# VectorE in place of TensorE for the small state space matrices of layer one

## The chip, the cores and the metric

One core of a Trainium2 chip runs the whole block. The metric is the device time in microseconds (us), median of the runs. TensorE (PE), VectorE (DVE), ScalarE (ACT), GpSimd (POOL) and the DMA queue of SyncE (SP) are five instruction streams that meet only at semaphores.

## The reference

One layer on 1024 positions of width 1024, all in float32:

```
x = x + 0.5 * swiglu(rms_norm(x, ff1_norm), w_gate, w_up, w_down)      # "layer one": FFN 1
h = rms_norm(x, mix_norm);  q, k, v, u = split(h @ w_in)
attn = banded_sink_attention(q, k, v, sink)
ssm:  lam_bar = exp(lam*dt);  b_bar = ((lam_bar - 1)/lam) * b         # 32 groups, 64 states, 16 channels
      states = scan(lam_bar, u @ b_bar);  y = Re(states @ c) + d*u;  gelu, GLU
x = x + concat(rms_norm(attn), rms_norm(ssm)) @ w_out
x = x + 0.5 * swiglu(rms_norm(x, ff2_norm), ...);  return rms_norm(x, final_norm)
```

The state space part is computed in 128 chunks of 8 positions. For it the kernel needs, out of the small parameters: the injection matrices E (b_bar times powers of lam_bar, one 128x128 matrix for each of 16 pairs of groups, real and imaginary), the output matrices CL (c times powers of lam_bar), and the rotation factors of each chunk (cosine and sine, `cs`).

## The kernel before

Every instruction's order is written out by hand, one list for each engine, with semaphores between them. Both FFNs are Strassen products: per FFN 8 opening quarters, then instances n = 2 to 21 of 7 products of 12 matmuls (3 for each operand tile: low times high, high times low, high times high), then `down` with 77 steps (7 products of 11 steps, 12 matmuls a step). ACT and DVE split each weight tile into a high and a low part ahead of its use, DVE also makes the Strassen sums. In `down` a ring of six slots is filled: at its step q DVE splits the tiles of step q + 4.

GpSimd does the small work beside FFN 1, in program order: its small loads (each parameter load waits for a certain product of TensorE), a chain of 128x16 operations for lam, then it waits for `ct_taken` and makes CL in 16 pieces that go to DRAM, then a loop of four batches. Each batch copies its operands to `cur`, computes E for four pairs into `EBb` (L3352 to L3354), a small operation `passed` (L3340), stores EBb to DRAM (L3356), waits for the landing, computes the rotation factors by doubling into the same EBb (L3359 to L3376), and stores them too (L3379). After the loop GpSimd adds the squares for the norm of the mixer (L3071), which `norm_sum(N_MIX, 0)` on TensorE (L1211) waits for at step 70 of `down`. ACT computes these squares, and takes the next one only when the add before last is done.

Turned matrices: c is turned by 8 TensorE transposes (`c_tiles`, L1386) before instance 10 and copied by ACT (`c_out`). E comes back from DRAM to `ebs` after FFN 1 in one load of SP (L1106) and is turned by 32 TensorE transposes (`transposes_e`, L1492) before input projections 4 and 5 of the mixer, and copied to `Et` by ACT (`e_out`, L2088). Projections run in the order IN_ORDER; `WITH_PE` and `WITH_ACT` say which small steps stand in front of, or in the middle of, which projection: K makes the kernel blocks, I injects (L1505, needs Et and u8), Y outputs. SP stores each tile of u and loads it back as `u8` (L1046) for the injection; the rotation factors `csn` (L1052) are loaded between these, each after a number of transposes of E.

Of the kernel before, what the change touches and what calls it, by code (L numbers as in the profile page):

```python
# [122 lines left out]
def taken_in(o):  # L123
# [7 lines left out]
WITH_PE = {(1, 1): steps("m1"), (4, 0): steps("E0 E1 E2 E3"), (5, 0): steps("E4 E5 E6 E7"), (6, 0): steps("K0"), (6, 1): steps("I0"),  # L131
# [3 lines left out]
WITH_ACT = {3: steps("e0 e1 e2 e3 W3"), 4: steps("e4 e5 e6 e7 W4"), 5: steps("k0 k1 W5"), 6: steps("k2 k3"),  # L135
# [18 lines left out]

ROUND = [((kind, 2 * b + i) if kind == "K" else (kind, b), 0 if kind == "K" else i)
         for kind, b in sum((WITH_PE[o] for o in sorted(WITH_PE)), []) if kind in "KEIY"
         for i in range(1 if kind == "E" else 2)]
# [266 lines left out]
def block_kernel(nc, x, ff1_norm, ff1_w_gate, ff1_w_up, ff1_w_down, mix_norm, w_in, sink, a_re, a_im,  # L424
# [85 lines left out]
    ebs = at("ebs", 64 * KB, [P, 2, NJ, P])  # L510
    csn = [at(f"csn{b}", (64 + 4 * b) * KB, [P, 2, 4, NC]) for b in range(4)]
# [7 lines left out]
    Et = at("Et", 162 * KB, [P, NJ, 2, P])  # L519
    Mt = at("Mt", 162 * KB, [P, NG, P])  # L520
# [48 lines left out]
    c_in = at("c_in", a_v + 2 * KB, [P, 2, 4, 2, NS])  # L569
    cl_st = at("cl_st", a_v + 2 * KB, [P, 2, 2, (T + 1) * GH])  # L570
    EBb = at("EBb", a_v + 2 * KB, [P, 2, 4, P])
    CT = at("CT", a_v + 6 * KB, [P, 2, NJ, GH])
    ptmp = at("ptmp", a_v + 8 * KB, [P, 2, 256])
    bc_tmp = at("bc_tmp", a_v + 8 * KB, [P, 2, NJ, GH])
# [74 lines left out]
    eb_d = nc.dram_tensor("eb_scratch", (P, 2, NJ, P), F32, kind="Internal").ap()  # L649
# [72 lines left out]
    ct_ready = sem("ct_ready")  # L722
# [6 lines left out]
    pool_chain = sem("pool_chain")  # L729
    eb_stored = sem("eb_stored")  # L730
    cl_stored = [sem(f"cl_stored{i}") for i in range(2)]
# [8 lines left out]
    eb_loaded = sem("eb_loaded")  # L740
# [4 lines left out]
    e_ready = sem("e_ready")  # L745
    e_taken = sem("e_taken")
# [94 lines left out]
    def _(sp):  # L841
# [263 lines left out]
        sp.wait_ge(eb_stored, 4 * 32 + 16)  # L1105
        sp.dma_start(ebs[:, :, :, :], eb_d).then_inc(eb_loaded, 16)  # L1106
# [12 lines left out]
        load_csn(1)  # L1119
# [62 lines left out]
    def _(pe):  # L1182
# [198 lines left out]
        def c_tiles():  # L1381

            pe.wait_ge(c_loaded, 64)
            for ri in range(2):
                for i in range(4):
                    last = nc.tensor.transpose(bank[6 + ri][:, i * P:(i + 1) * P],  # L1386
                                               c_in[:, ri, i, :, :].rearrange("p a s -> p (a s)"), ident[:, :])
                last.then_inc(ct_ready, 1)

# [52 lines left out]
        for n in range(2, N_INST):  # L1442
            if n == 10:
                c_tiles()
            instance(n)
        down(0, first_half(N_MIX))

        def round_free(kind, b, i=0):
# [11 lines left out]
            if kind == "K":  # L1460
                pe.wait_ge(k_taken, b + 1)
            elif kind == "E":
                pe.wait_ge(e_taken, b + 1)
# [21 lines left out]
        def transposes_e(b):  # L1485

            pe.wait_ge(eb_loaded, 16)
            round_free("E", b)
            for jj in range(2):
                for ri in range(2):  # L1490
                    m = 2 * jj + ri
                    last = nc.tensor.transpose(bank[round_bank("E", b)][:, m * P:(m + 1) * P],  # L1492
                                               ebs[:, ri, 2 * b + jj, :], ident[:, :])
            last.then_inc(e_ready, 1)

        def inject(b):

            pe.wait_ge(e_taken, 2 * b + 2)
# [108 lines left out]
        step = {"K": blocks_k, "E": transposes_e, "I": inject, "Y": outputs_y,  # L1607
# [139 lines left out]
    def _(act):  # L1747
# [216 lines left out]
        def ffn(w):  # L1964

            for n in range(N_INST * w + 2, N_INST * (w + 1)):
                if n == 10:
                    c_out()
                instance(n)
# [26 lines left out]

        def c_out():

            for ri in range(2):
                act.wait_ge(ct_ready, ri + 1)  # L2000
                for g2 in range(2):
                    r = slice(g2 * NS, (g2 + 1) * NS)
                    src = bank[6 + ri][r, :].rearrange("p (j g h) -> p g j h", g=2, h=GH)[:, g2]
                    act.activation(CT[r, ri, :, :], src, ACT.Copy).then_inc(ct_taken, 1)

# [58 lines left out]
        act.wait_ge(eb_stored, 4 * 32 + 16)  # L2064
# [18 lines left out]

        def e_out(b):
            act.wait_ge(e_ready, b + 1)
            if b == 0:
                wait_lo(act, 2 * KD)
            act.activation(Et[:, 2 * b:2 * b + 2, :, :],  # L2088
                           bank[round_bank("E", b)][:, :].rearrange("p (j r m) -> p j r m", j=2, r=2), ACT.Copy
                           ).then_inc(e_taken, 1)  # L2090
# [66 lines left out]
        step = {"k": k_out, "e": e_out, "y": y_out, "X": exponentials, "C": p_out, "O": o_out, "g": gelu,  # L2157
# [148 lines left out]
    def _(dve):  # L2306
# [341 lines left out]
        def instance(n):  # L2648
# [16 lines left out]

            ahead_sum(0)
# [4 lines left out]
            ahead(2)  # L2671
            gate_c12(n)
# [20 lines left out]

        def ffn(w):

            for n in range(N_INST * w + 2, N_INST * (w + 1)):
                if n == 7:
                    prepare()
                instance(n)
            down(w)  # L2700

        def x_out(t, kh=1):
# [3 lines left out]
                            ).then_inc(xt_dve, 1)  # L2706

# [354 lines left out]
    def _(pool):  # L3062
# [21 lines left out]
        def small_loads():  # L3084
# [31 lines left out]
        def load_c(n, a):  # L3116

            pool.dma_start(c_in[:, n, :, a, :], (c_re, c_im)[n][0].rearrange("(i g) h p -> (g h) i p", g=8)
                           ).then_inc(c_loaded, 16)
# [86 lines left out]
        tt(th, aim, dt, ALU.mult)  # L3206
        exp_parts(xr)
        load_b(1, 0)
# [42 lines left out]
        for k in range(1, T):  # L3251
            if k % 2:
                load_c(k // 4, k // 2 % 2)
# [50 lines left out]
        pool.wait_ge(ct_taken, 4)  # L3304
# [25 lines left out]
        with pool.Fori(0, NJ // 4) as i:  # L3330
# [7 lines left out]
            def passed():  # L3338

                pool.tensor_tensor(mark[:, :], unit[:, 0, 0, :], unit[:, 0, 0, :], ALU.mult)  # L3340

            pool.wait_ge(eb_stored, i * 32 + 16)
# [5 lines left out]
            q = [ptmp[:, n, 0:4 * GH].rearrange("p (j h) -> p j h", h=GH) for n in range(2)]  # L3348
# [12 lines left out]
            while n < NC:  # L3361
                v = [ptmp[:, m, 0:4 * n].rearrange("p (j c) -> p j c", j=4) for m in range(2)]
# [6 lines left out]
                if 2 * n < NC:  # L3369
                    a, b_ = ptmp[:, 0, 0:4], ptmp[:, 1, 0:4]  # L3370
# [121 lines left out]
```

## Time and profile before

| | us |
|---|---|
| median of 3 runs | 1590.37 (1590.2 to 1590.79) |
| profiled execution | 1590.72 |
| its span | 1588.9 |
| PE busy in it | 1580.6 |
| DVE busy | 1096.8 |
| ACT busy | 714.3 |
| POOL busy | 512.5 |

The span is the time from the first to the last instruction of the profiled execution. The granted TensorE clock is 1.00 in each stage, which is the 2.4 GHz level. FFN 1 lasts to about 654, the mixer to about 922, FFN 2 to the end. Times in rows are microseconds from the start of the span.

### The profile page before, as it was taken

To read this page: it belongs to the slowest core of one execution; us is meant where nothing else is said; L and a number is where in the kernel's file an instruction comes from. 1 tells how busy PE (TensorE), PEld (TensorE's weight loads), DVE (VectorE), ACT (ScalarE), POOL (GpSimd) and SP (SyncE) were. 2 spreads that over 40 slices of the span, in tenths; PEclk is the share of its full clock that TensorE was granted. 3 is DMA by queue.
4 is the path that set the end of the run, shared out by engine and by line. 5 is a ranking of instruction groups with operands and counts; after the bars stand their busy time and mean duration, and the time that the engine had idled before them with its cause. 6 is when DMAs were issued, how large, how long until landed. Compare 5 with 4: busy or idle time off the path is not lost.

```text
span 1588.9 us, 22029 instructions
## 1 busy us (share of the span) xinstructions
PE 1580.6 (99%) x7537; PEld 1305.3 (82%) x7537; DVE 1096.8 (69%) x1731; ACT 714.3 (45%) x1323; POOL 512.5 (32%) x938
## 2 busy tenths in 40 slices
PE   9999999999999999999999999999999999999998
PEld 7888888888888888888887888888888888888887
DVE  7966667766569886854369768766566666578766
ACT  7544343433334444532567544434344343344444
POOL 3005788877768778323030250000000000000000
PEclk9999999999999999999999999999999999999999
DMA  8253334433488545766631131433333333885443
GB/s 287 92 80 111 119 119 148 146 138 124 166 318 265 139 137 135 271 182 151 133 133 41 54 134 53 131 106 106 106 107 106 106 106 129 309 279 152 123 110 139
DMA packets 158455, 230.06 MB, mean 145 GB/s; under 512 B 25864, under 2 KB 95120, under 8 KB 154768
## 3 DMA queue, kind: packets, MB, share of 16 engines
q1 hardware_dynamic: 155120, 221.02, 43.6%
q0 software_dynamic: 3072, 7.62, 2.6%
q8 instruction: 61, 1.00, 0.3%
q14 instruction: 42, 0.34, 0.1%
q10 hardware_dynamic: 160, 0.07, 0.0%
HBM read 153.47 MB, written 74.15 MB: 143 GB/s over the span
## 4 chain that ended last, share of the span: by engine, by line
PE 98%; POOL 1%; ACT 0%; DMA 0%; DVE 0%; issue 0%; SPq 0%; DVEq 0%; POOLq 0%; ACTq 0%
PE bank L1185 31%; PE bank L1186 31%; PE bank L1187 31%; POOL ssq L3071 1%; PE bank L1552 1%; PE bank L1579 1%; PE bank L1534 0%; PE bank L1505 0%; PE bank L1479 0%; PE bank L1565 0%; PE bank L1527 0%; DMA x_in<-in_x_dram 0%; PE bank L1714 0%; PE bank L1219 0%; PE bank L1412 0%
## 5 line engine op out<-in xcount | busy, mean ns | idle before, releaser
L1185 PE MATMUL bank<-hbhi,ws_lo 128*128 128x512 f32 x1040 | 405.2, 390 | 0.0
L1187 PE MATMUL bank<-hbhi,ws_hi 128*128 128x512 f32 x1040 | 404.7, 389 | 0.0
L1186 PE MATMUL bank<-hblo,ws_hi 128*128 128x512 f32 x1040 | 404.6, 389 | 0.0
L1187 PEld LDWEIGHTS bank<-hbhi,ws_hi 128*128 128x128 f32 x1040 | 195.2, 188 | 40.7
L1185 PEld LDWEIGHTS bank<-hbhi,ws_lo 128*128 128x128 f32 x1040 | 195.2, 188 | 40.6 <-issue 0.4
L1186 PEld LDWEIGHTS bank<-hblo,ws_hi 128*128 128x128 f32 x1040 | 195.3, 188 | 40.3
L3071 POOL TENSOR_TENSOR ssq<-ssq,sqt 128x512 f32<-128x512 f32 x18 | 25.2, 1401 | 615.1 <-ACT sqt L1767 613.4
L1185 PE MATMUL bank<-d_hi,ws_lo 128*128 128x512 f32 x572 | 222.8, 389 | 0.0
L1187 PE MATMUL bank<-d_hi,ws_hi 128*128 128x512 f32 x572 | 222.5, 389 | 0.0
L1186 PE MATMUL bank<-d_lo,ws_hi 128*128 128x512 f32 x572 | 222.5, 389 | 0.0
L1837 ACT ACTIVATE loc<-bank 128x512 f32<-128x512 f32 x160 | 95.6, 597 | 251.6 <-PE bank L1187 251.6
L1884 ACT ACTIVATE d_hi<-d_in 128x512 fp32r<-128x512 f32 x154 | 96.0, 628 | 199.9 <-DMA d_in<-b_scratch 199.6
L2405 DVE TENSOR_TENSOR ws_lo<-w_sum,ws_hi 128x512 fp32r<-128x512 f32 x160 | 115.1, 719 | 97.3 <-ACT ws_hi L1800 97.3
L2575 DVE TENSOR_TENSOR d_lo<-d_in,d_hi 128x512 fp32r<-128x512 f32 x154 | 113.7, 740 | 82.9 <-ACT d_hi L1884 82.7
L1800 ACT ACTIVATE ws_hi<-w_sum 128x512 fp32r<-128x512 f32 x160 | 100.2, 626 | 76.2 <-PE bank L1187 60.1
L1185 PEld LDWEIGHTS bank<-d_hi,ws_lo 128*128 128x128 f32 x572 | 107.4, 188 | 22.7 <-issue 0.4
L1187 PEld LDWEIGHTS bank<-d_hi,ws_hi 128*128 128x128 f32 x572 | 107.4, 188 | 22.4
L1186 PEld LDWEIGHTS bank<-d_lo,ws_hi 128*128 128x128 f32 x572 | 107.4, 188 | 21.9
L1185 PE MATMUL bank<-hT_hi,w_lo 128*128 128x512 f32 x288 | 116.0, 403 | 0.0
L1186 PE MATMUL bank<-hT_lo,w_hi 128*128 128x512 f32 x288 | 112.4, 390 | 0.0
L1187 PE MATMUL bank<-hT_hi,w_hi 128*128 128x512 f32 x288 | 112.4, 390 | 0.0
L2405 DVE TENSOR_TENSOR ws_lo<-raw2a,ws_hi 128x512 fp32r<-128x512 f32 x78 | 55.0, 712 | 64.5 <-ACT ws_hi L1800 63.7
(319 smaller groups left out, 2696.6 us busy)
## 6 DMA issues: line engine op xcount, KB each, us to landing
b_scratch<-loc SPq DMA_DIRECT2D x42, 1024.0 KB, 7.3
d_in<-b_scratch SPq DMA_DIRECT2D x154, 256.0 KB, 3.1
raw2a<-in_ff_w_up_dram SPq DMA_DIRECT2D x42, 512.0 KB, 4.9
loc<-in_ff_w_gate_dram SPq DMA_DIRECT2D x36, 512.0 KB, 4.9
xT<-x_scratch SPq DMA_DIRECT2D x12, 1024.0 KB, 6.6
x_scratch<-xT SPq DMA_DIRECT2D x5, 2048.0 KB, 8.2
dw_lo_place<-in_ff_w_down_dram SPq DMA_DIRECT2D x8, 1024.0 KB, 7.9
x_in<-in_x_dram SPq DMA_DIRECT2D x8, 512.0 KB, 7.7
```

The lines of the kernel that those rows point to most:

```text
L1185: nc.tensor.matmul(o, wl, rh, start=first, stop=False, skip_group_check=chain)
L1186: nc.tensor.matmul(o, wh, rl, start=False, stop=False, skip_group_check=chain)
L1187: return nc.tensor.matmul(o, wh, rh, start=False, stop=last, skip_group_check=chain)
L1552: last = nc.tensor.matmul(o, qT[r, n, 2 * a:2 * a + 2, :].rearrange("p g q -> p (g q)"), kTp[r, n * CHUNK:n * CHUNK + P], start=True, stop ...
L1579: last = nc.tensor.matmul(bank[V_BANK[m]][kv * HD:(kv + 1) * HD, nn * 256:(nn + 1) * 256], vwin[:, 2 * m + nn, kv * HD:(kv + 1) * HD], pts ...
L1800: act.activation(as_block(ws_hi[b][:, :]), weights(n, s), ACT.Copy).then_inc(ws_hi_done, 1)
L1837: act.activation(snap[w][:, i, :], bank[inst_bank(n, role)][:, :], ACT.Copy).then_inc(snap_taken, 1)
L1884: act.activation(d_hi[q % N_SLOT][:, :], d_in[q % N_SLOT][:, :], ACT.Copy).then_inc(d_hi_done, 1)
L2405: dve.tensor_tensor(as_block(ws_lo[b][:, :]), weights(n, s), as_block(ws_hi[b][:, :].bitcast(F32)), ALU.subtract).then_inc(ws_lo_done, 1)
L2575: dve.tensor_tensor(d_lo[q % N_SLOT][:, :], d_in[q % N_SLOT][:, :], d_hi[q % N_SLOT][:, :].bitcast(F32), ALU.subtract).then_inc(d_lo_done, 1)
L3071: pool.tensor_tensor(ssq_of(norm, h), ssq_of(norm, h), sqt_of(norm, a), ALU.add).then_inc(ssq_done, 1)
```

## The change

VectorE turns c and E in blocks of 32x32, and what a full turn needs beyond that is done by the layout of the DMAs.

- c is loaded by 16 DMAs of 16 partitions and runs of 128 bytes in place of 4, and earlier in GpSimd's order (around `exp_parts(xr)` and no longer in the loop over k). DVE turns it in two instructions (`turn_c`) before its instance 8. TensorE's 8 transposes and ACT's copies are gone.
- In each of the four batches DVE turns EBb into a new tile EBt, two instructions of 128x512 (`turn_e`). GpSimd waits for them (`eb_turned`) and stores EBt by 4 DMAs of 32 partitions and runs of 128 bytes. It no longer waits for a store to land before the rotation factors. DVE does its turns at fixed places: before everything of instance 16; in instance 20 ahead of `gate_c12`; at step 21 and at step 52 of `down`. There it waits for `eb_made`.
- SP loads Et in 4 DMAs of 512-byte runs straight into its place; `ebs`, TensorE's 32 transposes and ACT's 8 copies are gone. The first two loads of rotation factors move ahead of `load_in(4)`.
- Et and Mt move to 64 KB, csn to 162 KB (they swap places); `csn` 2 waits for the norm's low parts. bc_tmp moves, ptmp has a second place in the loop.
- The parameter loads a_re, a_im and log_dt wait for earlier products: the last one for product 3 of instance 3 in place of product 3 of instance 4.

```diff
-WITH_PE = {(1, 1): steps("m1"), (4, 0): steps("E0 E1 E2 E3"), (5, 0): steps("E4 E5 E6 E7"), (6, 0): steps("K0"), ...
+WITH_PE = {(1, 1): steps("m1"), (6, 0): steps("K0"), ...
-WITH_ACT = {3: steps("e0 e1 e2 e3 W3"), 4: steps("e4 e5 e6 e7 W4"), ...
+WITH_ACT = {3: steps("W3"), 4: steps("W4"), ...
+E_TURN_INST = {16: (0, 0), 20: (1, 2)}
+E_TURN_STEP = {21: 2, 52: 3}
+E_STORES = 4 + 1
...
+    csn = [at(f"csn{b}", (162 + 4 * b) * KB, [P, 2, 4, NC]) for b in range(4)]
+    Et = at("Et", 64 * KB, [P, NJ, 2, P])
+    Mt = at("Mt", 64 * KB, [P, NG, P])
+    et_d = nc.dram_tensor("et_scratch", (32, NJ, 2, 4, P), F32, kind="Internal").ap()
...                                                            # SP
         def load_csn(b):
-            sp.wait_ge(e_ready, 4 if b == 0 else 8)
             if b:
                 sp.wait_ge(cs_loaded, 16 * b)
+            if b == 2:
+                wait_lo(sp, 2 * KD)
...
-        sp.dma_start(ebs[:, :, :, :], eb_d).then_inc(eb_loaded, 16)
+        for b in range(P // 32):
+            sp.dma_start(Et[32 * b:32 * b + 32, :, :, :], et_d[:, :, :, b, :]).then_inc(et_loaded, 16)
...
+        load_csn(0)
+        load_csn(1)
         load_in(4)
         store_u(0)
-        load_csn(0)
         load_u8(0)
         load_in(5)
         store_u(1)
-        load_csn(1)
         load_u8(1)
...                                                            # PE
-            if n == 10:
-                c_tiles()
...
         def inject(b):
-            pe.wait_ge(e_taken, 2 * b + 2)
+            pe.wait_ge(et_loaded, 64)
...                                                            # DVE
             for q in range(6 * N_PAIR):
+                if q in E_TURN_STEP and w == 0:
+                    turn_e(E_TURN_STEP[q])
...
+        def turn_e(b):
+            dve.wait_ge(eb_made, b + 1)
+            for ri in range(2):
+                dve.transpose(EBt[:, :, ri, :], EBb[:, ri, :, :]).then_inc(eb_turned, 1)
+        def turn_c():
+            dve.wait_ge(c_loaded, 16 * 16)
+            for ri in range(2):
+                dve.transpose(CT[:, ri, :, :]..., c_in[:, ri, :, :]...).then_inc(ct_taken, 1)
...                                                            # POOL
-                    pool.wait_ge(product_done, products(2 + n, 3 * g2))
+                    pool.wait_ge(product_done, products(2, 4 * n + 2 * g2))
-                pool.wait_ge(product_done, products(4, 3 * g2))
+                pool.wait_ge(product_done, products(3, 1 + 2 * g2))
...
+        load_c(0, 0)
+        load_c(0, 1)
         exp_parts(xr)
+        load_c(1, 0)
+        load_c(1, 1)
...
-            passed()
-            pool.dma_start(eb_d[:, :, bass.ds(i * 4, 4), :], EBb[:, :, :, :]).then_inc(eb_stored, 16)
-            pool.wait_ge(eb_stored, i * 32 + 32)
+            passed().then_inc(eb_made, 1)
+            pool.wait_ge(eb_turned, i * 2 + 2)
+            for a in range(P // 32):
+                pool.dma_start(et_d[:, bass.ds(i * 4, 4), :, :, 32 * a:32 * a + 32]..., EBt[32 * a:32 * a + 32]...
+                               ).then_inc(eb_stored, 16)
```

## Rows read from the trace of the kernel before

**Rows 1.** The page's busy times, and the waits of PE (in total, times, longest).

```profile
PE 1580.6 (99%) x7537; PEld 1305.3 (82%) x7537; DVE 1096.8 (69%) x1731; ACT 714.3 (45%) x1323; POOL 512.5 (32%) x938
...
PE bank L1211 <- POOL ssq L3071: 0.2, 1, 0.2
```

**Rows 2.** Timeline of PE where c is turned: start, duration, line, operands, count.

```profile
214.37 1.03 PE L1386 MATMUL bank<-ident,c_in 128*128 128x128 f32 x8
...
215.47 0.39 PE L1186 MATMUL bank<-hblo,ws_hi 128*128 128x512 f32 x1
```

**Rows 3.** Timeline of PE where E is turned, then the group by line.

```profile
676.97 0.39 PE L1187 MATMUL bank<-hT_hi,w_hi 128*128 128x512 f32 x1
677.20 1.91 PE L1492 MATMUL bank<-ident,ebs 128*128 128x128 f32 x16
...
679.18 0.39 PE L1186 MATMUL bank<-hT_lo,w_hi 128*128 128x512 f32 x1
...
L1492 PE MATMUL bank<-ident,ebs x32: 270/272/273, 677.2 to 686.1; 128*128 128x128 f32 x32
```

**Rows 4.** Timeline of POOL at the ends of batches, and its adds for the norm.

```profile
499.23 0.68 POOL L3356 DMA_DIRECT2D eb_scratch<-EBb  x1
503.16 0.84 POOL L3359 TENSOR_TENSOR EBb<-unit 128x8 f32<-128x8 f32 x1 [3.25 <-DMA eb_scratch<-EBb]
...
585.49 0.53 POOL L3340 TENSOR_TENSOR mark<-unit 128x1 f32<-128x1 f32 x1
...
590.32 0.69 POOL L3359 TENSOR_TENSOR EBb<-unit 128x8 f32<-128x8 f32 x1 [3.54 <-DMA eb_scratch<-EBb]
...
626.76 1.36 POOL L3071 TENSOR_TENSOR dw_hi_place<-dw_hi_place 128x512 f32<-128x512 f32 x1
...
631.68 1.57 POOL L3071 TENSOR_TENSOR dw_hi_place<-dw_hi_place 128x512 f32<-128x512 f32 x1
```

**Rows 5.** Timeline of PE at `norm_sum(N_MIX, 0)`.

```profile
634.46 0.60 PE L1211 MATMUL bank<-ident,dw_hi_place 128*128 128x128 f32 x4
```

**Rows 6.** Timeline of DVE around the four places where turns of E are put.

```profile
331.06 0.81 DVE L2387 TENSOR_TENSOR w_sum<-raw2a 128x512 f32<-128x512 f32 x1
...
415.20 0.69 DVE L2405 TENSOR_TENSOR ws_lo<-w_sum,ws_hi 128x512 fp32r<-128x512 f32 x1 [1.32 <-ACT ws_hi L1800]
...
502.05 0.68 DVE L2570 TENSOR_TENSOR ws_lo<-dw_lo_place,ws_hi 128x512 fp32r<-128x512 f32 x1
...
585.15 0.81 DVE L2570 TENSOR_TENSOR ws_lo<-dw_a,ws_hi 128x512 fp32r<-128x512 f32 x1
```

**Rows 7.** Groups by line: POOL's DMA issues (ns), and DVE's transpose of v.

```profile
L3356 POOL DMA_DIRECT2D eb_scratch<-EBb x4: 679/679/682, 341.4 to 586.1; - x4
...
L3113 POOL DMA_DIRECT2D b_raw<-in_b_im_dram x2 | 1.8, 894 | 1.2 <-POOL pw L3170 0.9 <-POOL pw L3166 0.3
...
L2799 DVE STREAM_TRANSPOSE vTp<-bank x2: 717/718/718, 743.8 to 753.2; 128x512 f32<-128x512 f32 x2
```

**Rows 8.** POOL's timeline after the parameter loads, and the page's DMAs (median us to landing).

```profile
130.81 0.82 POOL L3113 DMA_DIRECT2D b_raw<-in_b_re_dram  x1 [18.52 <-DMA par<-in_log_dt_dram]
...
b_raw<-in_b_re_dram POOLq DMA_DIRECT2D x2, 64.0 KB, 6.0
...
par<-in_log_dt_dram POOLq DMA_DIRECT2D x2, 4.0 KB, 17.6
```

**Rows 9.** The load of the second tile of u8, its injection on PE, and u8's landings.

```profile
691.29 4.50 SPq L1046 DMA_DIRECT2D u<-u_scratch  x8
...
701.41 1.97 PE L1505 MATMUL bank<-u,Et 128*64 128x128 f32 x32
...
DMA to landing us min/median/max: 2.0/2.6/4.3
```

**Rows 10.** Timeline of POOL: one operation of the loop beside an idle and a full DVE.

```profile
333.27 0.30 POOL L3353 TENSOR_TENSOR ptmp<-cur 128x64 f32<-128x64 f32 x1
...
579.75 0.63 POOL L3353 TENSOR_TENSOR ptmp<-cur 128x64 f32<-128x64 f32 x1
```

More of the change, by code:

```diff
@@ L152 @@
 STATE_STEPS = 4 * 5 + 8
+E_TURN_INST = {16: (0, 0), 20: (1, 2)}
+E_TURN_STEP = {21: 2, 52: 3}
+E_STORES = 4 + 1
 ROUND = [((kind, 2 * b + i) if kind == "K" else (kind, b), 0 if kind == "K" else i)
-         for kind, b in sum((WITH_PE[o] for o in sorted(WITH_PE)), []) if kind in "KEIY"
-         for i in range(1 if kind == "E" else 2)]
+         for kind, b in sum((WITH_PE[o] for o in sorted(WITH_PE)), []) if kind in "KIY"
+         for i in range(2)]
 def round_number(kind, b, i=0):
@@ L509, in block_kernel @@
     zT_lo = at("zT_lo", 48 * KB, [P, 4, L], F32R)
-    ebs = at("ebs", 64 * KB, [P, 2, NJ, P])
-    csn = [at(f"csn{b}", (64 + 4 * b) * KB, [P, 2, 4, NC]) for b in range(4)]
+    csn = [at(f"csn{b}", (162 + 4 * b) * KB, [P, 2, 4, NC]) for b in range(4)]
     yT = at("yT", 64 * KB, [P, 4, L])
@@ L729, in block_kernel @@
     pool_chain = sem("pool_chain")
+    eb_made = sem("eb_made")
+    eb_turned = sem("eb_turned")
     eb_stored = sem("eb_stored")
+    et_loaded = sem("et_loaded")
     cl_stored = [sem(f"cl_stored{i}") for i in range(2)]
@@ L1379, in x_tiles @@
                     last.then_inc(xt_done, 1)
[L1381 to L1388, printed above, removed]
         def first_half(norm):
@@ L1483, in blocks_k @@
                             last.then_inc(k_ready, 1)
[L1485 to L1494, printed above, removed]
         def inject(b):
-            pe.wait_ge(e_taken, 2 * b + 2)
+            pe.wait_ge(et_loaded, 64)
             pe.wait_ge(u8_loaded, 16 * T * (b + 1))
@@ L1605, in ssm_piece @@
             last.then_inc(mix_out, 1)
-        step = {"K": blocks_k, "E": transposes_e, "I": inject, "Y": outputs_y,
+        step = {"K": blocks_k, "I": inject, "Y": outputs_y,
                 "S": scores, "T": transposes_p, "V": weighted, "p": ssm_piece, "P": lambda i: ssm_piece(i, lambda: scores(i)), "m": lambda h: norm_sum(N_MIX, h), "n": lambda h: norm_sum(N_ATT, h),
@@ L1995, in x_out @@
                                ).then_inc(xt_act, 1)
[L1997 to L2004, printed above, removed]
         act.dma_start(ident[:, :], ident_c).then_inc(ident_loaded, 16)
@@ L2698, in ffn @@
                     prepare()
+                elif n == 8:
+                    turn_c()
                 instance(n)
@@ L2706, in x_out @@
                             ).then_inc(xt_dve, 1)
+        def turn_c():
+            dve.wait_ge(c_loaded, 16 * 16)
+            for ri in range(2):
+                dve.transpose(CT[:, ri, :, :].rearrange("p j h -> p (j h)"),
+                              c_in[:, ri, :, :].rearrange("p j s -> p (j s)")).then_inc(ct_taken, 1)
         def prepare():
@@ L3114, in load_b, with load_c @@
                            (b_re, b_im)[n][0].rearrange("(j g) p h -> g p j h", g=2)[g2]).then_inc(b_loaded, 16)
-        def load_c(n, a):
-            pool.dma_start(c_in[:, n, :, a, :], (c_re, c_im)[n][0].rearrange("(i g) h p -> (g h) i p", g=8)
-                           ).then_inc(c_loaded, 16)
+        def load_c(n, g2):
+            for sh in range(2):
+                for jj in range(2):
+                    q = 64 * g2 + 32 * sh + GH * jj
+                    pool.dma_start(c_in[q:q + GH, n, :, :],
+                                   (c_re, c_im)[n][0].rearrange("(j a g) h s -> a g h j s", a=2, g=2)[jj, g2][:, :, 32 * sh:32 * sh + 32]
+                                   ).then_inc(c_loaded, 16)
         def norm(which):
@@ L3347, in _ @@
                 ilink(pool.tensor_copy(cR[:, ri], rot8[:, ri, bass.ds(i * 4, 4)]))
-            q = [ptmp[:, n, 0:4 * GH].rearrange("p (j h) -> p j h", h=GH) for n in range(2)]
+            q = [ptmp_e[:, n, 0:4 * GH].rearrange("p (j h) -> p j h", h=GH) for n in range(2)]
             for t in range(T):
@@ L3361, in _ @@
             while n < NC:
-                v = [ptmp[:, m, 0:4 * n].rearrange("p (j c) -> p j c", j=4) for m in range(2)]
+                v = [ptmp_e[:, m, 0:4 * n].rearrange("p (j c) -> p j c", j=4) for m in range(2)]
                 w = [cR[:, m, :].unsqueeze(2).to_broadcast([P, 4, n]) for m in range(2)]
```

52 lines of the change are left out of this document (20 added, 32 removed).

## The prediction

> **What bounds the kernel now.** I read the page's busy times first. PE works 1580.6 us of a span of 1588.9 us, and the list of PE's waits has only one entry in the region of the change, 0.2 us for GpSimd's squares [rows 1]. So two questions decide: how much PE work goes, and whether anything that PE hardly waits for today becomes late. I then read PE's timeline at the removed transposes [rows 2, 3], and for each other engine the moment at which it hands over, against the moment at which PE asks [rows 4 to 6, 9].
>
> **What goes from PE.** The 8 transposes of c begin at 214.37, and the second matmul behind them at 215.47 [rows 2]. Without them it would begin one matmul spacing after 214.37. That spacing is 677.20 - 676.97 = 0.23 us [rows 3]. So they cost 1.10 - 0.23 = 0.87 us. For 16 transposes of E it is 679.18 - 677.20 - 0.23 = 1.75 us, and there are 32 [rows 3]: 3.50 us. Sum: 4.4 us. The mean duration of one (0.27 us) can't be used, as they overlap. ACT's 8 + 4 copies go too, worth nothing, since PE doesn't wait for ACT there.
>
> **What is added on DVE.** Eight transposes of 128x512 for E and two of 128x256 for c. The one of v took 0.72 us out of PSUM [rows 7]; back to back I take 0.65 each, so 1.3 us a batch. In the instances DVE has idle time (before the operation at 415.20 it sat 1.32 us waiting for ACT, [rows 6]), and in `down` the step it works on is used by PE four steps later. The work itself costs PE nothing. The waits of DVE for `eb_made` are the danger: behind the waiting turn stand all of DVE's splits, and behind these PE.
>
> **When GpSimd hands over.** The last parameter load moves by one instance (19 us by the spacing of instances, 7 x 12 x 0.23), and GpSimd stood 18.52 us for it before it went on at 130.81 [rows 8]. Sixteen loads of c in place of four cost it 7 to 10 us again (0.7 to 0.9 us an issue, [rows 7]). So it enters the loop some 10 us earlier, at least 7. The first batch was ready at 341.4 [rows 7] and would be at about 331; DVE arrives at 331.06 less the 0.9 us that PE has gained [rows 6]. From the first to the last batch GpSimd needs (586.1 - 341.4) / 3 = 81.6 us each [rows 7], and DVE's four places lie 84.8, 86.2 and 83.1 us apart [rows 6]. Thus DVE finds batches 1 and 2 ready, and GpSimd waits for DVE: it is from now on tied to DVE's places.
>
> **The last batch, step by step.** Turn 2 begins at 502.05 - 0.88 = 501.2, where GpSimd is ready at about 499.2 + 0.7, and ends at 502.5. Now come four store issues. The present one takes 0.68 us, one with 1024 short runs (b_raw) 0.89 [rows 7]: 2.7 to 3.8 us in all, and I take 3.0, nearer the store of the same loop. GpSimd begins the rotation factors at 505.6 where it did at 503.16 [rows 4]: 2.4 us later than before. Batch 3 would be made at 586.0 + 2.4 = 588.4 (585.49 and 0.53 for `passed`, [rows 4]). DVE is at its place at 585.15 - 0.88 = 584.3 [rows 6] and waits. While it waits, GpSimd's operations run at 0.30 in place of 0.63 us [rows 10]; with gaps and copies I take 1.6 times faster, so the last 4.1 us become 2.6 and the batch is made at 586.9. Turn 1.3, semaphore 0.1, stores 3.0: rotation factors from 591.3 where it was 590.32 [rows 4], 1.0 later. DVE then catches up and collides with GpSimd a little more, 0.3. So the adds for the norm begin 1.3 us later.
>
> **What that costs.** Four adds must be done before PE's `norm_sum`. They began at 626.76 and the fourth ended at 631.68 + 1.57 = 633.25 [rows 4]; PE came at 634.46 [rows 5]. The slack is 1.2 us, of which the earlier PE eats 0.9. So PE waits 1.3 - 0.3 = 1.0 us. Bounds: nothing, if the stores issue quickly and turns are short; and 4.1 us, with stores at 3.8 us and no gain in speed beside a waiting DVE (3.2 late after turn 2, 0.9 more at turn 3, 0.3 for collisions, less 0.3).
>
> GpSimd and VectorE slow each other here: the same operation of GpSimd took 0.30 us beside an idle DVE and 0.63 beside a full one [rows 10]. The Trainium skill (SBUF — State Buffer, Who interferes with whom) says that a VectorE instruction with two SBUF inputs contends with a reading GpSimd instruction, and one with a single SBUF input does not. By that rule the turns, with one input, take nothing from GpSimd, as in my sum; were it wrong, each batch would add at most the turns' 1.3 us to GpSimd, and only where GpSimd doesn't stand still for them anyway: the sum stays.
>
> **SP's queue.** Et comes in four loads where one stood, with CL and an input tile behind them. The projections asking for these lie 20 us off, so nothing. Rotation factors 0 and 1 leave the stretch between the u8 loads. The second tile of u8 was issued until 691.29 + 4.50 = 695.8 and lands 2.6 us after its issue, so at 698.4, and PE injected at 701.41 [rows 9]. PE now comes at 697.0. If the queue did not move, it would wait 1.4 us; but the two csn loads no longer stand in it and its own trigger, a projection of PE, moves as well, so I expect it 2 to 4 us earlier. Cost 0, bounds 0 and 1.4; the tiles behind it are alike, and a wait at one gives the others time.
>
> **Sum.** Profiled execution 1590.7 - 4.4 + 1.0 = 1587.3; it lay 0.35 above the median of the runs. Against that median: 1590.37 - 3.4 = **1587.0**. After the mixer nothing changes, and all of it is paced by PE.
>
> **Rivals.**
> - *Full gain.* GpSimd's adds are ready in time. For it: 1.2 us of slack today, and a DVE that waits speeds GpSimd up. Against: the four issues. 1586.0. Chance 0.30.
> - *The gain is given back.* Stores at 3.8 us, no speeding up, or waits for u8: 3 to 4.4 us of PE waits, 1589 to 1590.4. For it: in the last batches DVE is full beside GpSimd [rows 10]. Chance 0.17.
> - *Slower: the short stores hold the loop.* GpSimd enters the next batch only when all five stores of the last one have landed. The DMA of 1024 single values took 17.6 us to land, that of 1024 runs of 64 bytes 6.0 [rows 8]. If each of the four stores took 17.6 in turn, 70 us would pass where about 41 are there (36.4 us of rotation factors from 590.32 to 626.76, [rows 4], and some 5 for a landing), 29 us too much a batch; about 11 us are caught at the turns, and DVE, waiting at its places, would keep PE waiting: some 60 us, 1650. It decides from about 45 us for the four together; at 50 us it is 3 x 9 less what slack catches, some 16 us, and 1602. Against it: 4 x 6.0 = 24 us by the nearer row. A second way to this side is a first batch that comes 6 us late at instance 16, if the parameters land late. Chance 0.10.
> - *The change doesn't do what it says:* the transposes go in any case, and PE is nowhere idle beside them; I give it nothing.
>
> A rule that speaks for the slow side: the Trainium skill (DMA: Bandwidth & Descriptors, its table of figures at the head) wants at least 512 bytes a run and says that below it the DMA engine reads, modifies and writes. The new stores have 128. The trace has no such store; by the rule they'd be slower than today's store of 2 KB runs, which is the rival above.
>
> **Chances and range.** My own case (a wait of 0.4 to 3 us) has 0.43. Faster by over 0.2% means below 1587.2; 0.2% is about what a measurement of this kernel tells from no change. That holds for the full gain and for half of my case: 0.51. Slower (above 1593.5): 0.10. Within: 0.39. The range goes from 1585.6 (full gain, 0.4 for noise and easier queues) to 1591.2 (both bounds of the waits together, 4.1 and 1.4, would give 1591.5).
>
> **What would show it.** Right: no PE rows with `ident,ebs` or `ident,c_in`; two DVE STREAM_TRANSPOSE rows at each of four places near 330, 415, 501 and 587; GpSimd standing some 9 us before the second store, little before the others; DVE waiting 2 to 3 us for GpSimd at the last turn; the first add for the norm at about 628, and a wait of PE at its transposes for `norm_sum` of about 1 us. Wrong: a first add before 627 with no PE wait (full gain), or PE waits at an instance of FFN 1, at `inject`, or GpSimd's loop waiting over 8 us for stores to land.

## The result: slower, and by two waits of TensorE

| us | before | after |
|---|---|---|
| median of the runs | 1590.53 (1590.2 to 1590.79) | 1601.18 (1600.11 to 1603.34) |
| profiled execution | 1590.72 | 1600.11 |
| its span | 1588.9 | 1598.4 |

The ratio is 1.0069, with a 95% interval of 1.0056 to 1.0081. The prediction was 1587.0, in a range of 1585.6 to 1591.2. The profiled execution of the changed kernel is the fastest of its four runs; the account below is of that one, 9.4 us above before, where the medians lie 10.65 apart. The transposes are gone and PE's busy time is the same, which already says that some of the remaining work ran slower. PE's waits, the answer to [rows 1], name two places (in total, times, longest; "issue" means that the profile names nothing that PE waited for):

```profile
PE 1580.6 (99%) x7497; PEld 1304.6 (82%) x7497; DVE 1102.5 (69%) x1741; ACT 709.5 (44%) x1311; POOL 525.7 (33%) x962
...
PE bank L1218 <- POOL dw_hi_place L3056: 5.6, 1, 5.6
PE bank L1488 <- issue: 4.1, 1, 4.1
```

L1218 is `norm_sum` (L1211 before), L1488 is `inject` (L1505 before; `inject(b)` needs tile b of u8), L1473 makes the kernel blocks. PE's timeline around both, for [rows 5] and [rows 9]:

```profile
632.88 0.39 PE L1194 MATMUL bank<-d_hi,ws_hi 128*128 128x512 f32 x1
638.86 1.12 PE L1218 MATMUL bank<-ident,dw_hi_place 128*128 128x128 f32 x4 [5.59 <-POOL dw_hi_place L3056]
...
640.20 0.63 PE L1193 MATMUL bank<-d_lo,ws_hi 128*128 128x512 f32 x1
640.63 0.63 PE L1194 MATMUL bank<-d_hi,ws_hi 128*128 128x512 f32 x1
...
642.75 0.39 PE L1193 MATMUL bank<-d_lo,ws_hi 128*128 128x512 f32 x1
642.97 0.39 PE L1194 MATMUL bank<-d_hi,ws_hi 128*128 128x512 f32 x1
...
699.27 1.97 PE L1488 MATMUL bank<-u,Et 128*64 128x128 f32 x32
...
708.32 3.68 PE L1488 MATMUL bank<-u,Et 128*64 128x128 f32 x32 [4.13 <-issue]
711.93 3.10 PE L1473 MATMUL bank<-CL,Bb 64*16 64x128 f32 x32
```

Behind each wait the work runs at half speed for a while: matmuls 0.43 us apart until 642.3 and 0.23 from 642.75 on; an injection of 3.68 us where the one before it took 1.97. The stretches by time show it as the granted clock (the number behind the brackets; 0.5 is the 1.2 GHz level, 1.00 the 2.4 GHz level; the rows are the stretch behind each wait and the one after that):

```profile
638.80:643.00 4.20, 4.14 (x13) 3.45 (x14) 3.54 (x6) 3.01 (x7) 2.91 (x3) 0.53 0.01 2
643.00:647.00 4.00, 4.00 (x22) 3.30 (x20) 3.90 (x9) 3.67 (x7) 1.37 (x2) 1.00 0.48 124
...
708.30:715.00 6.70, 6.68 (x65) 5.46 (x65) 4.69 (x11) 0.00 (x0) 4.62 (x4) 0.55 0.64 176
715.00:719.00 4.00, 4.00 (x25) 3.11 (x25) 3.79 (x12) 0.96 (x2) 3.56 (x7) 1.00 0.89 222
```

With the start times of the same steps of PE in both timelines the whole difference comes apart (after less before, at each step):

| step on PE | before | after | difference | what happened since the step above |
|---|---|---|---|---|
| norm_sum(0) | 634.46 | 638.86 | +4.40 | c gone: -0.88 (measured in e14_sp_order below), wait: +5.28 |
| norm_spread(0) | 640.37 | 646.62 | +6.25 | lower clock: +1.85 |
| first kernel block | 691.73 | 694.43 | +2.70 | E gone: -3.55 |
| inject(1) | 701.41 | 708.32 | +6.91 | wait: +4.21 |
| inject(2) | 708.79 | 718.59 | +9.80 | lower clock: +2.89 |
| span | 1588.9 | 1598.4 | +9.5 | nothing of note |

So the gain of 4.4 us is there in full. Against it stand 9.5 us of waits, and 4.7 us of a halved clock behind them. (`norm_spread`, L1226, is the next step of the norm.)

**Why GpSimd was late.** Its timeline at the two last turns, for [rows 4], and the group of its store issues, for [rows 7]:

```profile
503.62 3.31 POOL L3349 DMA_DIRECT2D et_scratch<-EBt  x4 [3.67 <-DVE EBt L2668]
506.94 0.22 POOL L3353 TENSOR_TENSOR EBb<-unit 128x8 f32<-128x8 f32 x1
...
586.51 0.20 POOL L3331 TENSOR_TENSOR mark<-unit 128x1 f32<-128x1 f32 x1
588.75 1.62 POOL L3349 DMA_DIRECT2D et_scratch<-EBt  x2 [2.04 <-DVE EBt L2668]
594.31 1.56 POOL L3349 DMA_DIRECT2D et_scratch<-EBt  x2 [3.94 <-issue]
595.88 3.02 POOL L3353 TENSOR_TENSOR EBb<-unit 128x8 f32<-128x8 f32 x1
...
633.00 7.49 POOL L3056 TENSOR_TENSOR dw_hi_place<-dw_hi_place 128x512 f32<-128x512 f32 x5
...
L3349 POOL DMA_DIRECT2D et_scratch<-EBt x16 | 12.8, 804 | 18.4 <-DVE EBt L2668 14.0 <-issue 4.3
```

Up to 586.7 the timetable of the prediction holds. Then two things come that it has no term for: 3.94 us between the second and the third store, in which GpSimd waits for nothing that the profile names, and an operation of 128x8 that takes 3.02 us (0.69 before). The adds for the norm begin at 633.00.

**Why u8 was late.** SP's timeline, and the wait in it:

```profile
660.88 4.87 SPq L1113 DMA_DIRECT2D Et<-et_scratch  x4
...
671.26 14.30 SPq L1058 DMA_DIRECT2D csn<-cs_scratch  x2
685.61 0.60 SPq L851 DMA_DIRECT2D raw<-in_w_in_dram  x1
686.26 0.57 SPq L1041 DMA_DIRECT2D u_scratch<-ust  x1
693.37 3.64 SPq L1051 DMA_DIRECT2D u<-u_scratch  x8
...
702.73 3.63 SPq L1051 DMA_DIRECT2D u<-u_scratch  x8
...
SPq L1058 <- DMA csn<-cs_scratch: 12.4, 1, 12.4
```

`load_csn(b)` waits until csn b-1 has landed. Behind the four loads of Et (2 MB together), CL (2.3 MB), an input tile and 1 MB of parked x, csn 0 is waited for during 12.4 us, and the store of u, the input tile and both u8 loads stand behind that wait. The second u8 tile went out from 702.7 on (691.3 before, [rows 9]), though PE was to come earlier.

### The profile page after: what moved, and what is told of

The parts are those of the page before. It is cut to its first block, busy times and chain, and to the rows that moved or that the text cites. A ratio compares the mean times of both kernels' runs of the same rounds, so it can differ in the third digit from the quotient of the medians.

```text
span 1598.4 us, 21991 instructions
## 1 busy us (share of the span) xinstructions
PE 1580.6 (99%) x7497; PEld 1304.6 (82%) x7497; DVE 1102.5 (69%) x1741; ACT 709.5 (44%) x1311; POOL 525.7 (33%) x962
## 4 chain that ended last, share of the span: by engine, by line
PE 89%; POOL 6%; issue 2%; DMA 1%; POOLq 0%; DVE 0%; ACT 0%; SPq 0%; DVEq 0%; ACTq 0%
PE bank L1192 28%; PE bank L1194 28%; PE bank L1193 28%; POOL EBb L3362 1%; POOL ptmp_e L3361 1%; POOL ptmp_e L3360 1%; PE bank L1488 1%; PE bank L1535 1%; POOL ptmp_e L3343 1%; PE bank L1473 1%; POOL EBb L3345 1%; POOL ptmp_e L3344 1%; PE bank L1562 1%; PE bank L1517 0%; PE bank L1548 0%
```

## Experiments

Theory A: a VectorE that has waited at a turn catches up without a gap and starves GpSimd. Theory B: the wait of csn 1 for csn 0 in SP's queue makes u8 late. Their rivals: the four issues stall by themselves; the four loads of Et are what is late.

**Turn 3 a step later**

```diff
-E_TURN_STEP = {21: 2, 52: 3}
+E_TURN_STEP = {21: 2, 53: 3}
```

> The changed kernel with its last turn of E one step of `down` later (53 for 52). In the trace of the changed kernel DVE waited 2.8 us there, then worked 10.8 us without a gap, and in that stretch GpSimd stood 3.94 us between its second and third store and took 3.02 us for an operation of 128x8. Theory A: a VectorE that catches up without a gap starves GpSimd. At 53 DVE waits at most 1.3 us, catches up less, the two stalls shrink from 6.2 us together to under 3; the first add for the norm comes at 628 to 630 (633.0 in the changed kernel), PE waits 1 to 3 us at norm_sum (5.6): 1595.5 to 1598 us. Rival: four store issues in a row are what stalls (a queue that takes two). Then the 3.9 us gap stays, the first add comes at 631.5 or later and the time is at least 1599.5.

Measured: 1598.46 us (1596.81 to 1601.41), ratio to before 1.0056 [1.0039, 1.0073]. VectorE waited 1.2 us at its turns in all (4.1 in the changed kernel), the gap between store 2 and 3 stayed at 3.48 us, the first add came at 631.56. That is 1.4 us earlier than in the changed kernel, as the first operation behind the stores took 1.68 for 3.02 us. Theory A fails for the stall: the longer operation behind it may still be VectorE's doing. The time lies between the two ranges that were expected.

**csn 1 back**

```diff
         load_csn(0)
-        load_csn(1)
         load_in(4)
...
         store_u(1)
+        load_csn(1)
         load_u8(1)
```

> The changed kernel with the second load of rotation factors (csn 1) back behind store_u(1), as before the change. In the trace of the changed kernel SP stood 12.4 us for the landing of csn 0 before it could issue csn 1, and load_in(4), store_u(0), both u8 loads behind it. Theory B: this wait in the queue makes inject(1) wait 4.1 us, and the halved clock after it costs 2.9 more: without it u8 tile 1 is issued before 696, no PE wait at any inject, 7.0 us less: 1594 us (1593 to 1595). Rival: the four loads of Et (4.9 us of issue where one took 0.3) and their lateness are the cause: then inject(1) still waits 3 us or more and the time is 1598 or more.

Measured: 1594.50 us (1593.05 to 1598.64), ratio 1.0029 [1.0019, 1.0040], 6.7 us less than the changed kernel. inject(1) waits no more. New are 0.3 us at inject(2) and 1.4 us at inject(3). Theory B holds; the four loads of Et are still there, and inject(1) does not wait for them. Not all of the 6.7 us is this edit's. By the profiled runs, the changed kernel loses 6.8 us against before behind its first kernel block and this one 1.8, so 5.0 us are the edit's. The other 1.8 us lie ahead of that block, at norm_sum, which the edit doesn't touch: GpSimd's adds began at 631.33 here and at 633.00 there.

**Both**

> Both edits: turn 3 at step 53, csn 1 back. If both theories hold, and their effects add: 1588.5 to 1591 us, PE's only wait in the region that at norm_sum, 1 to 3 us. If either rival holds, 1592 or more.

Measured: 1594.46 us (1593.07 to 1596.15), ratio 1.0026 [1.0015, 1.0038], no better than csn 1 back alone, and above the 1588.5 to 1591 us that both theories together would give. GpSimd still stalled for 3.56 us; PE waited 3.1 us at norm_sum and 2.1 us at inject(3).

**VectorE only waits, in the kernel before**

```diff
+                if q == 51 and w == 0:
+                    dve.wait_ge(ct_taken, 4 + 4)
...
-            passed()
+            passed().then_inc(ct_taken, 1)
             pool.dma_start(eb_d ...
```

> The kernel before, in which DVE only waits, ahead of step 51 of `down`, until the last batch of E is made, some 3 to 4 us; no turn, one store as before. Theory A (a DVE that catches up starves GpSimd): DVE then works without a gap for over 8 us, GpSimd shows one or two idle stretches or operations of over 2 us in it, the first add for the norm comes at 628 or later (626.8 before) although the batch itself is made 1 to 1.5 us earlier, PE waits 1 us or more at norm_sum: 1591.5 to 1594. Rival (the four store issues stall by themselves): GpSimd has no such stretch, the first add comes at 625 to 626.5, time 1590.2 to 1590.8.

Measured: 1590.63 us (1590.30 to 1591.19), ratio 1.0001 [0.9991, 1.0010]. It tested nothing: in the profiled run GpSimd had made the last batch at 581.6, and VectorE shows no wait for it, though the same code made it at 586.0 in the kernel before. That is a finding of its own: GpSimd's loop is over 4 us earlier or later in one build than in another that gives it the same work, and the slack of 1.2 us that the prediction counted is one draw. A second pair shows it too: the changed kernel and e2_csn1_back differ only in SP's order from 671 us on, and the first batch was made at 331.3 and at 325.1. Some 4 us of this is one wait for a store of CL to land (6.81 us and 2.81) just ahead of the loop.

**One issue more, four issues less, 1024 runs more, code moved**

```diff
 e5: d_skip loaded in two halves in place of one
 e6: +pool.dma_start(par[:, n, :], a[0].rearrange("(j g) p -> (g p) j", g=2)), b likewise; turn 3 at 53, csn 1 back
 e10: +pool.dma_start(spare[:, :], a_re[0].rearrange("(j g) p -> g p j", g=2)[0])
 e11: +for _ in range(6): ilink(pool.tensor_tensor(ptmp_e[:, 0, 0:1], ...))      # ahead of the stores
```

> The changed kernel in which one small early load of GpSimd (d_skip, at 36 us) is split into two: one DMA issue of GpSimd more, everything else alike. In all traces with the turns GpSimd stands 3.5 to 3.9 us before the third store of the last batch, which is its 80th DMA issue (20 small loads and zero stores, 6 parameters, 4 of b, 16 of c, 16 of CL, 5 a batch, 2). Theory C: GpSimd's DMA issue number 80 has to wait until the ones just before it have landed. Then the stall moves to between the first and the second store of the last batch, and keeps its 3.5 to 4.5 us. Rivals (a VectorE without gaps; the place in the code; the bytes or runs issued so far, which don't change): the stall stays between the second and the third store.

> Turn 3 at step 53 and csn 1 back (as in e3_both), and GpSimd's two loads each of a_re, a_im, b_re and b_im made into one each: four issues of GpSimd fewer, the same bytes and runs. Theory C (by count): the last batch never reaches the 80th issue, no idle stretch over 1 us between its stores, the first add for the norm comes at 626.5 to 628.5 (631.0 in e3_both), PE waits under 1 us at norm_sum and its clock stays at the upper level; inject(3) still waits 1.5 to 2.5 us: 1587.5 to 1590 us. Rivals (by runs, by place, by VectorE): the 3.6 us stall stays, 1593 us or more.

> The changed kernel with one more early load of GpSimd of 1024 single values into an unused place, so that 1024 more runs have passed through its queue before the last batch. Splitting a load with no more runs did not move the stall, nor did four issues fewer with the same runs. Theory D' (a ring that holds so many runs, and waits at its end for those on the way): the stall moves one store (1024 runs) up, to between the first and the second store of the last batch, at 3.5 to 4.5 us. Rival (place in the code, or the state of the other engines at that moment): it stays between the second and the third.

> The changed kernel with six small operations of GpSimd more ahead of the first store of each batch (0.2 to 0.6 us each, 2 to 3.5 us a batch). Theory F (GpSimd waits for its own instructions: a boundary in the code lies between the second and the third store): the stall of 3.5 to 4 us moves to an earlier place in the order, before the second store or ahead of it. Theories of the queue (runs, landing): it stays between the second and the third store.

Measured (one run each; e6 ten): 1600.67; 1594.05 (1592.19 to 1595.89, ratio 1.0020 [1.0010, 1.0029]); 1598.12; 1602.18 us. In all four the stall lay between the second and the third store of the last batch, and nowhere else: 4.17, 3.27, 3.68 and 3.82 us. So theory C (the 80th issue), theory D' (a ring that fills up by runs, as far as single values count in it) and theory F (a boundary in GpSimd's code) fall for this stall. e11 also shows what a late GpSimd costs: add at 636.03, a wait of 8.1 us. The median of e6 is 0.4 us below that of e3_both, far less than either spreads (3.7 and 3.1 us); what GpSimd wins is lost again at its turns, where it now waits for VectorE for 23.7 us in all (14.0 in the changed kernel).

**Wide runs**

```diff
-                pool.dma_start(et_d[:, bass.ds(i * 4, 4), :, :, 32 * a:32 * a + 32].rearrange("c j r b s -> c (j r b) s"), ...
+                pool.dma_start(et_d[:, bass.ds(i * 4 + a, 1), :, :, :].rearrange("c j r b s -> c (j r b s)"),
+                               EBt[32 * a:32 * a + 32, :, :, :].rearrange("c j r m -> c (j r m)")
```

> The changed kernel with GpSimd's four stores a batch in runs of 4 KB in place of 128 bytes (same four issues, same bytes; the blocks land in the wrong order, so the output matrix E is not the reference's). Theory D (the number of short runs decides): no stall before the third store of the last batch (3.5 to 4.2 us in all traces so far), landing as quick or quicker, first add for the norm 3 to 4 us earlier than the 632.6 to 633.0 us of the changed kernel. Rival (place in the code, or a VectorE without gaps): the stall stays at 3.5 us or more.

Measured (one run): 1592.61 us. GpSimd's timeline in this run, and its group of issues:

```profile
588.09 2.27 POOL L3349 DMA_DIRECT2D et_scratch<-EBt  x4 [2.00 <-DVE EBt L2668]
...
626.80 8.17 POOL L3056 TENSOR_TENSOR dw_hi_place<-dw_hi_place 128x512 f32<-128x512 f32 x5
...
L3349 POOL DMA_DIRECT2D et_scratch<-EBt x16 | 8.2, 511 | 23.1 <-DVE EBt L2668 22.1
```

No gap between the stores, an issue of 0.51 in place of 0.80 us, the first add at 626.80, and no wait at norm_sum. (The 4.2 us at inject(1) remain, since csn 1 is where the change put it.) The short runs are a condition of the stall (with them the issues are longer too, so which of the two counts is not shown). They also take longer to land: 4.1 us in the middle against 3.2.

The Trainium skill (DMA: Bandwidth & Descriptors, the table of figures at its head) asks for runs of at least 512 bytes. Here 128-byte runs did cost, but at the engine that issues them, and only a little in the landing; the rival that took landings of 17.6 us, from the row of single values, was off by four times.

**As many short runs more as a batch has**

```diff
+        for a in range(P // 32):
+            for jh in range(2):
+                pool.dma_start(et_d[:, 2 * jh:2 * jh + 2, :, :, 32 * a:32 * a + 32] ..., Bb[32 * a:32 * a + 32, ...] ...
```

> The changed kernel with 4096 more short runs of 128 bytes (eight stores of 512 runs, to places that the first batch overwrites) issued by GpSimd just ahead of its loop: as many as a batch has. With wide runs the stall was gone; extra issues, extra single values and shifted code did not move it. Theory G (short-run stores fill something up, and the 14th thousand of their runs meets its end): the stall of 3.5 to 4 us now lies in batch 2 (near 505 us), between its second and third store, or thereabouts, and none is at 590 us. Rival H (what counts is the moment near 590 us: what else is in the queues and on VectorE, with short runs): it stays in the last batch. VectorE may wait for the first batch here, so the time is of no use (1600 to 1612 us).

Measured (one run): 1599.91 us. The stall stayed in the last batch (3.53 us, 591.0 to 594.55). Theory G falls. A much smaller gap does move. In the changed kernel GpSimd stands 0.32 us before the second store of the second batch; with a batch's worth of short runs more (this run), the same gap lies before the second store of the first batch:

```profile
417.93 2.34 POOL L3349 DMA_DIRECT2D et_scratch<-EBt  x3 [0.32 <-issue]
...
336.77 2.33 POOL L3356 DMA_DIRECT2D et_scratch<-EBt  x3 [0.31 <-issue]
```

One issue more or four less (e5, e6) leave it where it was. With 1024 single values more (e10) it is gone from there, and the first store of that batch begins 0.5 us later (417.29 for 416.76), one store earlier. So this gap, and not the stall, goes by the number of runs, single values included; it costs 0.3 to 0.5 us once.

What the changed kernel's trace does show is when the stall ends. The DMA rows of 592.5 to 593.5, then those of 593.5 to 595.0 (q0 is GpSimd's queue; packets, MB, share):

```profile
q0 software_dynamic: 27, 0.05, 15.6%
...
q1 hardware_dynamic: 137, 0.25, 61.7%
```

The last packets of the first two stores pass by 593.5, from then on q0 is empty, and the third store is issued at 594.31. It is the same in all ten traces with the stall: the last packet of GpSimd's queue passed 0.75 to 1.5 us before the third store was issued. In batch 2, in contrast, the third store was issued while nearly all packets of the first two were still to come. GpSimd thus goes on when its own queue has run dry. The stall also moves with the stores: they began between 586.8 and 595.0 in these kernels, and it came each time 1.6 us later.

**Turns placed by GpSimd's needs; then the stores on SP's queue**

```diff
 e7 (on e6): +turn 1 after ahead(1) in place of ahead(2);  E_TURN_STEP = {20: 2, 52: 3}
 e12 (on e7): -GpSimd's stores of EBt
+        def store_et(b):                                                       # SP
+            sp.wait_ge(eb_turned, 2 * b + 2)
+            for a in range(P // 32):
+                sp.dma_start(et_d[:, 4 * b:4 * b + 4, :, :, 32 * a:32 * a + 32]..., EBt[32 * a:32 * a + 32]...).then_inc(et_stored, 16)
+        # after pair 18, the first group for `down`, steps 26 and 58;  DVE waits for et_stored, 64 * b, before turn b
```

> As e6, with turn 1 two VectorE operations earlier in instance 20 (after its second weight), turn 2 at step 20, turn 3 at step 52. GpSimd stood 6.2 and 3.7 to 5.7 us for these turns. It should be some 2.7 us earlier from turn 1 on. Theory: no PE wait at norm_sum, first add at 624 to 626.5; the only PE wait left is at inject(3), 1.5 to 2.5 us, without a drop of the clock: 1587 to 1588.5 us. If VectorE has to wait at an earlier place instead, first add as in e6 and the same time as e6.

> As e7_turns_earlier, with the four stores of E a batch issued by SP's queue in place of GpSimd (after pair 18, after the first group for `down`, after steps 26 and 58). GpSimd loses 3.3 us of issue a batch and the stall of 3.5 us. Theory: first add for the norm at 623 (ACT's squares set it), no PE wait at norm_sum, clock never halved there; what is left is inject(3), 1 to 2.5 us: 1586.5 to 1588 us, a spread of the runs under 1.5 us (6.3 us in e7). Rival: 5 us of issue in SP's queue in `down` make d_in late, and PE waits there: 1589 or more.

Measured: e7 1590.63 us (1587.43 to 1593.71), ratio 1.0001 [0.9992, 1.0011]. GpSimd was 1.9 us earlier at its last stores than in the changed kernel (586.81), stalled for 3.45 us all the same, and PE waited 2.3 us, where no wait was expected: as fast as before the change, but with a spread of 6.3 us. VectorE sat idle for 0.54 us in the middle of this stall (590.29 to 590.83), and GpSimd did not go on: one more sign against theory A. e12: 1587.67 us (1586.48 to 1590.10), ratio 0.9981 [0.9972, 0.9991], first add at 623.96, no wait at norm_sum. The runs still spread by 3.6 us, where under 1.5 was expected. SP takes 2.7 to 3.3 us for the four stores of batches 1 to 3 (7.2 for batch 0), and no load for `down` came late. What was left is at inject(3), here in its profiled run (1590.10 us, the slowest of ten):

```profile
723.43 2.83 PE L1503 MATMUL bank<-u,Et 128*64 128x128 f32 x32 [2.12 <-issue]
```

**SP's order around the last tile of u**

```diff
-        load_csn(3)
         store_k(0)
         load_in(6)
+        load_csn(3)
+        store_u(3)
+        store_k(1)
         load_m(0)
-        store_k(1)
-        store_u(3)
-        load_in(7)
         load_u8(3)
+        load_in(7)
         load_m(1)
```

> As e12_sp_stores, with SP's queue reordered around the last tile of u: csn 3, store_u(3) and store_k(1) ahead of the first load of M, load_in(7) behind the last load of u8. In e12 SP issued the last u8 tile at 717.3 to 720.9, though u was ready at 709.6, and inject(3) waited 2.1 us and ran at a lower clock for 0.9. Theory: the tile is issued 1 to 1.5 us earlier, inject(3) waits under 1 us: 1586 to 1587.2 us, median of e12 less 0.5 to 1.5. Rival: the moved load_in(7) or load of M makes a later projection or output wait: 1587.7 or more.

Measured: **1586.43 us** (1585.53 to 1588.17), ratio to before 0.9974 [0.9964, 0.9984]: 4.3 us less than 1590.75, the median of before beside it. It is faster than both kernels. u8's last tile goes out from 714.96 on (717.31 in e12), and the list of PE's waits has nothing left in the region. GpSimd's and PE's timelines:

```profile
585.45 0.56 POOL L3366 TENSOR_TENSOR EBb<-unit 128x8 f32<-128x8 f32 x1 [3.77 <-DVE EBt L2686]
...
623.79 6.29 POOL L3074 TENSOR_TENSOR dw_hi_place<-dw_hi_place 128x512 f32<-128x512 f32 x4
```

```profile
633.58 0.60 PE L1233 MATMUL bank<-ident,dw_hi_place 128*128 128x128 f32 x4
...
687.32 1.92 PE L1488 MATMUL bank<-CL,Bb 64*16 64x128 f32 x32
...
720.93 1.97 PE L1503 MATMUL bank<-u,Et 128*64 128x128 f32 x32
```

Against before, norm_sum is 634.46 - 633.58 = 0.88 us earlier and the first kernel block 691.73 - 687.32 = 4.41: the prediction's term for c (0.87) and its sum of both terms (4.4), measured without the waits.

**Only the c half, on the kernel before**

> The kernel before with only the c half of the change: c loaded by 16 small DMAs and turned by VectorE in two instructions, parameter loads earlier; E stays with TensorE. By the prediction's term for c, 0.87 us less: 1589.7 us (1589.4 to 1590.0), no new PE wait, since GpSimd is 15 us or more earlier in its loop and nothing ties it to VectorE. Rival: the 16 loads or the earlier parameters disturb instance 8 or the opening of FFN 1: not below 1590.5.

Measured: 1589.25 us (1589.03 to 1589.54) against 1590.56 (1590.23 to 1592.14); the runs do not overlap, the interval of the ratio, 0.9983 to 1.0002, just includes 1. The 1.3 us are somewhat more than 0.87, and just past the range of 1589.4 to 1590.0 that was expected; in the profiled runs norm_sum is 0.79 us earlier and the span 1.0 shorter. GpSimd, not tied to VectorE, is through with its loop at 609 and then waits for ACT's squares:

```profile
623.27 5.87 POOL L3057 TENSOR_TENSOR dw_hi_place<-dw_hi_place 128x512 f32<-128x512 f32 x4 [14.16 <-ACT dw_hi_place L1755]
```

## Why the prediction was wrong, step by step

- *What goes from PE* (0.87 + 3.50 us): right, 0.88 and 3.55.
- *What is added on DVE* (1.3 us a batch, free of cost): right. The turns took 1.29 to 1.30, and PE's list of waits has no new entry in FFN 1 ahead of norm_sum.
- *When GpSimd hands over*: right. It was in the loop at 301.59 (311.06 before), its first batch was ready at 331.3. VectorE waited 1.3 us for it at the first turn and 2.8 at the last; at the two between, GpSimd stood 6.2 and 3.7 us.
- *The last batch*: turn 2 began at 501.63 (501.2 predicted), its stores took 3.3 us (3.0), batch 3 was made at 586.7 (586.9). That last agreement is partly luck: the rotation factors began at 506.94, not at 505.6, and GpSimd was that much quicker over the rest. Here it failed: "Turn 1.3, semaphore 0.1, stores 3.0: rotation factors from 591.3". From the end of the turn to the first store 0.7 us passed, and the stores took until 595.88, since GpSimd stood 3.94 us in their midst; the first rotation operation then took 3.02 us. Rotation factors from 595.88, not 591.3, and adds from 633.0, not 628. I multiplied the duration of a single issue by four; that an issue can wait for the queue no row of before could show, since there each store was waited for before the next.
- *"0.3 for collisions"*: undersized. Operations of 128x4 to 128x64 that start while VectorE goes on without a gap took 2.44 us before (at 506.36), 3.02 after, 2.79 in e5, 3.14 in e13 and 3.28 in e4; seven more in all traces took 1.0 to 2.1, and the rest 0.2 to 0.9. Why just these are long is not shown. The row of 2.44 us stood in the trace of before and I did not read it.
- *What that costs*: 1.0 us forecast, 4.1 as the bound, 5.28 measured. And the term has no clock in it. PE lost another 1.35 to 2.9 us behind each wait at norm_sum of 2.3 us or more (the time from norm_sum to norm_spread, less that of before): 1.64 us behind a wait of 2.3 (e7), 1.35 behind 4.1 (e1), 2.88 behind 4.1 (e6), 1.85 behind 5.6 (after), 2.14 behind 8.1 (e11). It doesn't grow in step with the wait; it is rather a fee than a share. The prediction priced every wait without it. The Trainium skill (TensorE: Matmul & The Clock Gate, What's actually happening) names the two levels and says that the low one is where the clock rests and that activity lifts it; the traces agree (0.53 to 0.55 behind the waits of the changed kernel, 1.00 in the stretches after that, with PE busy throughout).
- *SP's queue*: this is the step that failed worst: "but the two csn loads no longer stand in it ... so I expect it 2 to 4 us earlier. Cost 0, bounds 0 and 1.4". They stood there still, only further ahead, one waiting for the landing of the other, 12.4 us, with everything else behind. It cost 4.2 us and 2.9 of clock. Even without this mistake (e2, e3, e12) the chain of u8 was late at inject(3) by 1.4 to 2.1 us: the last tile of u8 goes out at 717.31 in e12 and at 717.11 before, though PE is 4 us ahead. Part of this is links that wait for a landing (the stored kernel blocks, the stored u), part is SP's order: in e12 the tile of u was ready at 709.6 and SP came to store it at 713.36, behind loads of M. The new order of e14 brought the tile out 2.35 us earlier. A wait of that size I had named as a bound (1.4 us, for the second tile) and then counted as nothing.
- *In sum*: the profiled execution took 12.8 us more than the 1587.3 forecast for it: 4.3 more of wait and 1.85 of clock at norm_sum, 4.2 and 2.9 at inject(1), less some 0.4 of small differences.
- *Rivals*: "The gain is given back" had both mechanisms, wrongly sized, and a chance of 0.17. "Short stores hold the loop" had the right part and the wrong price: 4.1 us of landing, not 17.6. "After the mixer nothing changes, and all of it is paced by PE" was right: the difference is 9.80 us at inject(2) and 9.5 at the end.

## What to carry to other kernels

Where a load moves in a hand-written queue, take its waits along: what counts is not its 0.6 us of issue but what it waits for at the new place, and everything that then stands behind it. Where PE gets faster in front of a chain of DMAs, each waiting for the last to land, don't count on the chain getting faster with it; here its slack shrank by nearly the whole gain. Price a wait of TensorE with what the clock costs behind it: here 1.3 to 2.9 us behind every wait of 2.3 us or more, while of two waits of 2.1 us one cost nothing (e3, inject(3)) and one 0.9 us at the injection alone (e12).

And where GpSimd is close to the path, leave the DMAs with many short runs to a queue that has time: the same four stores cost GpSimd 3.2 to 7.1 us on the path, and SP 2.7 to 7.2 with nobody waiting.

## What was not expected of the hardware

- GpSimd stood 3.3 to 4.2 us before the third of four stores of 1024 runs of 128 bytes, in all ten profiled kernels that had them on GpSimd, only in the last of four like batches, and until its queue was empty. With runs of 4 KB it did not. Why only in the last batch stays open: the number of issues, 1024 single values more, 4096 runs more, six instructions more and a start 8 us earlier or later did not move it, and batch 2 had a VectorE just as full and DMA engines fuller (a share of 1.00 against 0.62), without it.
- SP issued the same stores of the last three batches at 0.7 to 0.8 us each and showed no such stall there; in the first batch one of its issues took 4.87 us.
- GpSimd's chain varies by over 4 us between kernels that give it the same work (the last batch made at 586.0 and at 581.6, the first at 331.3 and at 325.1). That fits the spread of the runs, 6.3 us in e7, where PE waits for GpSimd, and 0.5 in e8, where GpSimd is 14 us early. It isn't shown to be the cause: only one run of each kernel has a trace, and e12 spreads by 3.6 us with no such wait in its trace.
